# A fused decoder step on one core: weight loads placed three projection steps ahead of their splits in SyncE's order

## The reference

```python
h = rmsnorm(x, norm_in_w)
u = h @ w_in                      # 1024 -> 11792 columns, in one combined projection
y_ssd = ssd(z, conv(xBC), dt)     # causal conv(4) + SiLU, 16 heads x 64, chunked scan of 128 tokens, gated norm
y_att = dilated_attention(q, k, v)  # 3 groups x 8 heads x 64, windows 128/512/2048, dilations 1/4/16; * silu(z)
y_mem = cross_attention(q_mem, kv(rmsnorm(mem) @ w_mem_kv))   # 4 heads x 128 over 256 tokens; * silu(z)
merged = g0 * (y_ssd @ w_br_ssd) + g1 * (y_att @ w_br_att) + g2 * (y_mem @ w_br_mem)   # g = sigmoid(gates of u)
y = rmsnorm(x + merged @ w_out, norm_f_w)
```

## Time and profile before

| | |
|---|---|
| median of three runs | 2109.82 us |
| the profiled execution | 2112.42 us |
| its span | 2110.6 us |
| PE busy | 1979.0 us, 94% |
| DVE busy | 985.8 us |
| ACT busy | 765.1 us |
| mean granted clock of TensorE | 0.965 |

### The profile page before, as it was taken

One profiled execution on the slowest core, in us unless ns is written; L12 is line 12 of the kernel. 1 busy time (PEld: TensorE's weight loads), 2 busy tenths in 40 slices (PEclk: granted clock), 3 DMA queues, 4 the chain that ended last, 5 costly groups with the idle time before them and its releaser, 6 DMA issues.

```text
span 2110.6 us, 34859 instructions
## 1 busy us (share of the span) xinstructions
PE 1979.0 (94%) x14301; PEld 1892.0 (90%) x14301; DVE 985.8 (47%) x1941; ACT 765.1 (36%) x1642; POOL 242.0 (11%) x358
## 2 busy tenths in 40 slices
PE   5999999999989999999999899999999669969997
PEld 5899999999989999999999889669999659969997
DVE  5303676535465354443337684013555455454523
ACT  5223444323353333332655223115556532133202
POOL 1000111100001010112212100001211111100000
PEclk9999999999999999999999999998999879989999
DMA  6311332311112121212256784764545635554422
GB/s 216 92 42 52 93 93 83 93 46 40 49 33 65 41 67 39 87 44 90 86 170 198 237 260 141 268 228 134 169 153 161 216 88 179 175 173 140 143 84 104
DMA packets 171742, 257.18 MB, mean 122 GB/s; under 512 B 20229, under 2 KB 115269, under 8 KB 171557
## 3 DMA queue, kind: packets, MB, share of 16 engines
q1 hardware_dynamic: 149328, 187.97, 28.4%
q0 software_dynamic: 22256, 66.98, 9.4%
HBM read 188.13 MB, written 66.76 MB: 121 GB/s over the span
## 4 chain that ended last, share of the span: by engine, by line
PE 85%; DVE 5%; ACT 4%; DMA 3%; issue 2%; SPq 0%; POOL 0%; DVEq 0%; ACTq 0%; POOLq 0%
PE bank L2296 21%; PE bank L2297 21%; PE bank L2298 21%; PE bank L2496 3%; PE bank L2469 2%; PE bank L2452 2%; PE bank L2711 2%; PE bank L2600 1%; PE bank L2430 1%; DVE w_lo L1762 1%; PE bank L2755 1%; PE bank L2533 1%; DMA sums<-sum_T 1%; PE bank L2395 1%; PE bank L2394 1%
## 5 line engine op out<-in xcount | busy, mean ns | idle before, releaser
L2296 PE MATMUL bank<-w_hi,hT_hi 128*128 128x256 f32 (+1 forms) x1848 | 536.9, 291 | 0.2 <-issue 0.2
L2297 PE MATMUL bank<-w_lo,hT_hi 128*128 128x256 f32 (+1 forms) x1848 | 524.6, 284 | 0.0
L2298 PE MATMUL bank<-w_hi,hT_lo 128*128 128x256 f32 (+1 forms) x1848 | 523.6, 283 | 0.0
L2296 PE MATMUL bank<-hT_hi,w_hi 128*128 128x352 f32 x1344 | 451.3, 336 | 6.3 <-DVE acc L2143 5.7
L2298 PE MATMUL bank<-hT_hi,w_lo 128*128 128x352 f32 x1344 | 439.1, 327 | 0.0
L2297 PE MATMUL bank<-hT_lo,w_hi 128*128 128x352 f32 x1344 | 438.8, 327 | 0.0
L2296 PEld LDWEIGHTS bank<-w_hi,hT_hi 128*128 128x128 f32 (+1 forms) x1848 | 349.8, 189 | 1.9 <-issue 0.5
L2298 PEld LDWEIGHTS bank<-w_hi,hT_lo 128*128 128x128 f32 (+1 forms) x1848 | 350.6, 190 | 0.6
L2297 PEld LDWEIGHTS bank<-w_lo,hT_hi 128*128 128x128 f32 (+1 forms) x1848 | 349.7, 189 | 1.3
L2296 PEld LDWEIGHTS bank<-hT_hi,w_hi 128*128 128x128 f32 x1344 | 257.8, 192 | 20.1 <-issue 8.6
L2297 PEld LDWEIGHTS bank<-hT_lo,w_hi 128*128 128x128 f32 x1344 | 258.8, 193 | 0.5
(11 more groups left out here) (423 smaller groups left out, 2934.6 us busy)
## 6 DMA issues: line engine op xcount, KB each, us to landing
w_raw<-in_w_in SPq DMA_DIRECT2D x96, 512.0 KB, 5.0
kvring<-in_cache_win_kv SPq DMA_DIRECT2D x98, 256.0 KB, 4.8
feat_T<-fstage POOLq DMA_DIRECT2D x40, 528.0 KB, 4.2
fstage<-feat_T SPq DMA_DIRECT2D x16, 528.0 KB, 4.2
xc<-feat_T SPq DMA_DIRECT2D x8, 1024.0 KB, 5.9
sums<-sum_T SPq DMA_DIRECT2D x32, 256.0 KB, 4.5
o_rows<-obuf POOLq DMA_DIRECT2D x48, 132.0 KB, 2.0
mo<-o_rows SPq DMA_DIRECT2D x24, 264.0 KB, 3.3
```

Source lines behind the costliest of these rows:

```text
L2296: pe.matmul(out, xh(k), wh(k), start=(k == 0), stop=False)
L2297: pe.matmul(out, xh(k), wl(k), start=False, stop=False)
L2298: ins = pe.matmul(out, xl(k), wh(k), start=False, stop=(k == nk - 1))
```

## The change

At the end of `plan()` a step `("weights", n)` is put into the list for every `("split", n)`. Its place is found by walking back from the split over three projection steps, and the walk stops earlier if it comes to `("low", n - 1)`, behind which the raw buffer is free. SyncE issues the load of chunk n+2 at `weights` and no longer at `split`. The wait on `s_wlo` before the load stays as it was. The other engines do nothing at `weights`, so their orders don't change. There is no step `("low", -1)`, so for `("split", 0)` the walk takes its three projection steps in any case.

```diff
+WEIGHTS_AHEAD = 3
...
+    for n in [s[1] for s in sched if s[0] == "split"]:
+        at = sched.index(("split", n))
+        left = WEIGHTS_AHEAD
+        while left and sched[at - 1] != ("low", n - 1):
+            at -= 1
+            left -= sched[at][0] in ("tok", "feat", "p1", "p2", "out")
+        sched.insert(at, ("weights", n))
     return chunks, sched, units, sets, values, part_end
...
-                elif s[0] in ("load0", "split"):
+                elif s[0] in ("load0", "weights"):
                     n = s[1] if s[0] == "load0" else s[1] + 2
                     if n >= n_chunks:
                         continue
                     if n >= 1:
                         sp.wait_ge(s_wlo, n)
                     for i, src in enumerate(wsrc(n)):
                         sp.dma_start(w_raw[:, 4 * i:4 * i + 4, :], src).then_inc(s_w, 16)
```

## The result

The changed kernel takes 2126.1 us in the median (2123.8 to 2128.6, 4 runs) where the kernel before takes 2109.6 (2105.3 to 2115.6, 4 runs): a ratio of 1.0085, 95% interval 1.0065 to 1.0106, that is 17.9 us slower (13.7 to 22.4). A second comparison, run with the experiments, gave 1.0078 (1.0052 to 1.0103), 16.4 us. The forecast had the sign, 2120.8 us as the time and 2126.0 as the upper end of its range, which the median passes by 0.1 us. The forecast is too small by 5.3 us if the medians are compared and by 6.9 us if the ratio is.

A forecast was written before the change was run, and what follows sets the result against it. PE was taken as the bound, busy 94% of the span, so only what feeds it counts. Start 9.0, keys 0, values 1.7 + 0.3, SSD -0.3, output +0.3 sum to 11.0 us on 2109.82: 2120.8 us, range 2112 to 2126.

The forecast's parts named there:

- the sign: Whole kernel: slower by over 0.3%, given a chance of 0.76.
- Start, +9.0: Start: input row 7 is held behind chunk 2's load, delaying PE; 9.0 us slower, bounds 6.4 and 9.5.
- the tell-tales: Signs for the profile after, at the start: row 7 behind the weight load, square about 48.8, PE gap about 6 us.
- the growth behind the stand: Start: after standing idle 6.4 us PE returns at the lower clock, adding 2.6 us, between 0 and 3.1.
- Chunk 53, 0: SSD stage: chunk 53's load is moved past nothing, so PE's 12.4 us gap stays; value 0.
- SSD end opens: Rival at the SSD end: the 12.4 and 16.9 us gaps close, 29.3 us, giving 2091.5 us; chance 0.05.
- SSD, branches, output, 0: Late stages: SSD -0.3 us from shorter ACT waits, branches and output +0.3 from chunk 57 ahead of `yb` loads.
- Values, +2.0: Value loads: chunk 44 costs 0, chunk 45 +1.7 and chunk 46 +0.3 us.
- chunk 45 at 1.7: Values: chunk 45's load in front of value loads 36 to 47 costs 1.7 us, ends 0 and 5.0.
- the 5.0 us of the upper end: Values: chunk 45's cost if a whole DMA counts, the whole megabyte passing before the value loads.
- Chunk 44, which I set at 0: Values: `weights 42` holds value loads 0 to 5 until about 1313, but they land in time; 0, up to 3 us.
- Merge and keys, 0 between -0.5 and +1: Merge and key loads: chunks 38 and 40 to 42 go ahead, each costing about 1 us of issue; 0 in total.

The follow-up runs named there:

- e1: Kernel before with only chunk 2's load moved, to before input row 7: ratio 1.0046, +9.7 us.
- f4: Kernel before with only chunk 53's load moved, to right behind the lo half of chunk 52: ratio 0.9989, 2.3 us faster.
- g4: Kernel before with f4's place for chunk 53 and chunk 1's load put behind input row 6: ratio 0.9949, 10.7 us faster.
- f3: Kernel before, no load moved, but input row 7's load waits for the lo half of chunk 1: ratio 1.0024, +5.0 us.
- h2: Kernel before with only the loads of chunks 47 to 63 moved: ratio 1.0012.
- g3: Kernel before with only chunk 45's load moved, in front of value loads 36 to 47: ratio 1.0011.
- f2: The kernel before repeated unchanged: ratio 1.0007.
- h3: Kernel before with only chunk 41's load moved, in front of the first key loads: ratio 1.0008.
- e3: Kernel before with only the loads of chunks 41 and 42 moved, ahead of key loads: ratio 1.0000.
- g2: Kernel before with only the loads of chunks 2, 41, 42, 44, 45 and 46 moved: ratio 1.0065, +13.7 us.
- e2: Kernel before with all loads moved but chunk 2's: ratio 1.0018, +3.8 us.
- g1: Kernel before with all loads moved except those of chunks 2, 41, 42, 44, 45 and 46: ratio 1.0016, +3.4 us.

## Why the prediction was right or wrong

*Start, +9.0: right, with the clock's part set too high.* Measured +8.3 over the traces, 9.7 by e1's times. Row 7 behind the load at 41.99 (worked out 42.65), square at 48.14 (48.8), PE's gap 6.09 us (6.4), all as the tell-tales said. PE's transposes of row 7 are 5.6 us late (6.4) and the lo half of chunk 2 is 7.2 late (61.64, not the 63.4 forecast). So the growth behind the stand, for which I had put 2.6 us, is 1.6 us. On average the delay is 7.8 us at split 2 and 8.3 at split 10. The 9.6 us at split 10 between the first two profiles are 1.3 more than that, which is within the scatter: from split 2 to 10 the traces without the move alone differ by 4 us, and their granted clock by 0.96 to 0.99. From split 10 to 40 the delay stays whole.

*Chunk 53, 0: right.* Gap of 11.5 and 16.9 us where 12.4 and 16.9 had stood. That this rested on the list was shown by f4: a load really placed earlier does cut the gap. The rival "SSD end opens" valued both gaps at 29.3 us; f4 and g4 show that only some 6 of them go with the load. The Trainium skill, "DMA: Bandwidth & Descriptors", Rules for kernel authors, advises to issue a DMA early and to wait on it late. Chunk 53 in f4 and g4 agrees with it, a load that can be issued at once: PE's 12.4 us gap shrinks by some 6. e1, 9.7 us slower, shows the case in which the early issue itself has to wait, and f3, 5.0 us slower, has that wait alone.

*SSD, branches, output, 0: not contradicted.* ACT's waits for weights fell from 25.5 to 16.2 us and bought nothing, as forecast. h2's +2.5 us has 0 inside its interval.

*Values, +2.0: mis-sized.* +3.4 in the traces, without overlap. Value loads 0 to 5 are issued from 1331.83 on, which is the 1313 of the prediction plus the shift of 19 us. I put chunk 45 at 1.7, and g3's one trace has +2.0. The megabyte does pass first (the first value tile lands behind both of its halves), and yet the stage doesn't lose the 5.0 us of the upper end: most of it is covered. How the rest is shared between chunks 44, 45 and 46 isn't shown. Chunk 44, which I set at 0, may have a part: with its load moved, value loads 0 to 8 fall into the stage too, which by length and rate then moves 29 MB and not 27. The longest gap on value loads in the changed kernel, at 1403, is 1.88 us long:

```profile
1403.19 1.70 PE L2608 MATMUL bank<-kvring,pm_late 128*32 128x512 f32 x4 [1.88 <-DMA kvring<-in_cache_win_kv]
```

It can't be put down to the moved loads: at the same place f4, in which no load of the values moves, has a gap of 1.44 us, and the second trace of the changed kernel one of 0.48.

*Merge and keys, 0 between -0.5 and +1: the step that failed most clearly.* I counted 1 us of issue in front of loads "whose tiles PE uses some 10 us later" and never counted the megabyte itself, nor asked what state the DMA engines are in. SyncE as it ran:

```profile
1175.13 1.81 SPq L1110 DMA_DIRECT2D w_raw<-in_w_in  x2
1176.98 3.79 SPq L1169 DMA_DIRECT2D kvring<-in_cache_win_kv  x6
```

The DMA engines are nearly full in this stretch even before the change (0.87 to 1.05 in f2). So the key loads start 1 to 2 us later and land in full DMA engines: the first tile takes 6.5 us from issue to landing in the changed kernel and 7.6 in h3, where it takes 4.6 and 3.5 us in the two traces of the kernel before. PE's idle time grows by 0 to 1 us, and the stage takes 0.5 to 1.1 us more where the clock held, which is what my upper end allowed. In the other half of the traces the clock drops and the stage takes 3.4 to 3.9 us more, and for that the sum had no term. That is +2.2 on average from split 40 to 41, eleven traces against six, without overlap. In the times of e3 (0.0 us, -3.2 to 3.2) and h3 (+1.7, -1.9 to 5.5) alone it can't be told from 0.

*What stays open.* 8.3 + 2.2 + 3.4 = 13.9 us are tied to named loads, 2.9 more than the forecast of 11.0, and g2's 13.7 us, with chunk 42's load moved too, agrees. So the keys' 2.2 us and the 1.4 us too little in the values, less 0.7 too much at the start, are the part of the miss that is traced. The whole change measured 16.4 and 17.9, e1 and e2 together 13.5, g1 3.4 with no wait behind it. The remaining 2.5 to 4 us may be chunk 42's load (+2.9 in the table, with overlap, though the times of e3 show nothing of it), the clock falling in more places, or the loads behind the values. The intervals, each some 3 us wide to either side, don't decide.

## What to carry to other kernels

An early place in an issuing queue is only early if nothing ahead of it waits longer: a load that waits on a semaphore holds every load listed behind it, and here one such wait on an input row cost 4 to 5 us and the megabyte in front of it about as much again. Before moving a load, look at which engine's gap it closes (ACT's shorter waits were worth nothing) and at how full the DMA engines are where it lands. The same reading backwards found the gain: put what is ready in front of what waits, and move the one load whose gap PE really has.

## What was not expected of the hardware

The granted clock of the same stretch, with the same instructions in the same order and nearly the same idle time of PE, differs between executions: 0.85 to 0.94 from split 42 to 43 (58.8 us in g1, 54.2 in e1, in neither of which the loads there move) and 0.84 to 0.88 from 53 to 56 (177.9 and 183.5 us for the kernel before alone). Between split 40 and 41 the full clock held eleven times out of eleven with the old order and three times out of six with the new one, at idle times of PE that overlap; what tips it isn't shown here. A single profile of this kernel so carries 5 us of chance, which exceeds most of the terms that were summed.
